# Weight sums of the Winograd product made ahead and kept in DRAM, operand low parts on GpSimd, operand sums on VectorE

## What is computed

```python
def sq_relu_mlp(h, w1, w2):
    return jnp.square(jax.nn.relu(h @ w1)) @ w2

xl = xl + g2_l * sq_relu_mlp(modulate(rms_norm_2(xl, norm2_g[i]), sh2_l, s2_l),
                             mlp_w1[i], mlp_w2[i])
return rms_norm_2(xl, final_g)
```

## Time and profile before

| | us |
|---|---|
| median of 3 runs | 2065.61 (2061.8 to 2067.92) |
| the profiled execution, its own time | 2060.92 |
| its span on the core | 2058.9 |
| TensorE, matmuls, busy | 1984.6 |
| VectorE / ScalarE / GpSimd busy | 1236.4 / 861.5 / 924.2 |
| second product, groups 0 to 6 | from 1667.4 to 2002.8 |

### The profile page before, as it was taken

The page is one execution under the profiler, slowest core; times in us unless marked ns, Lnnn a source line. Parts: engine busy times, 40 slices in busy tenths (PEclk is TensorE's granted clock), DMA queues, the critical chain, the costliest instruction groups (busy, mean ns, idle before and its releaser), DMA issues.

```text
span 2058.9 us, 26605 instructions
## 1 busy us (share of the span) xinstructions
PE 1984.6 (96%) x10042; PEld 1658.4 (81%) x10042; DVE 1236.4 (60%) x2117; ACT 861.5 (42%) x1431; POOL 924.2 (45%) x562
## 2 busy tenths in 40 slices
PE   9999999999999999999999999999999998888897
PEld 7988988988988888888878877787888876666676
DVE  6255355536554455554789978974402058888866
ACT  5433332253435513122465575756445443333321
POOL 4512111221122335344279856883447466666621
PEclk9999999999999999999999999999999999999998
DMA  4301101111113677684354423443354432222222
GB/s 184 103 21 52 52 21 62 42 42 42 37 47 108 227 274 271 218 295 132 113 187 181 174 93 120 127 141 124 108 180 152 139 133 87 82 82 92 82 92 82
DMA packets 82814, 247.11 MB, mean 120 GB/s; under 512 B 9328, under 2 KB 9712, under 8 KB 82560
## 3 DMA queue, kind: packets, MB, share of 16 engines
q1 hardware_dynamic: 59504, 202.94, 29.0%
q10 hardware_dynamic: 23184, 42.48, 5.7%
...
## 4 chain that ended last, share of the span: by engine, by line
PE 51%; DVE 8%; issue 4%; POOL 3%; ACT 2%; DMA 1%; POOLq 0%; DVEq 0%; ACTq 0%
PE B L1711 34%; PE B L1890 9%; PE B L1941 5%; DVE RES L2478 2%; DVE OPL L2475 2%; DVE SUMR L2475 2%; DMA RAW<-wall 1%; POOL WL L3041 1%; POOL SUML L3046 1%; PE B L2016 1%; DVE HB L2478 1%; PE B L1952 0%; POOL CO L3107 0%; POOL OPT L3057 0%; DVE B L2478 0%
## 5 line engine op out<-in xcount | busy, mean ns | idle before, releaser
L1711 PE MATMUL B<-HB,WH 128*128 128x512 f32 x2976 | 948.9, 401 | 4.9 <-ACT HB L2141 2.2
L1711 PEld LDWEIGHTS B<-HB,WH 128*128 128x128 f32 x2976 | 547.6, 189 | 127.0 <-issue 17.1
L3041 POOL TENSOR_TENSOR WL<-RAW,WH 128x1024 fp32r<-128x1024 f32 x160 | 389.6, 2439 | 457.8 <-ACT WH L2141 367.4
L1711 PE MATMUL B<-HB,WL 128*128 128x512 f32 x1488 | 578.2, 391 | 1.0 <-POOL WL L3041 1.0
L2141 ACT ACTIVATE WH<-RAW 128x1024 fp32r<-128x1024 f32 x201 | 210.8, 1054 | 297.1 <-DMA RAW<-wall 267.2
L1711 PEld LDWEIGHTS B<-HB,WL 128*128 128x128 f32 x1488 | 280.0, 188 | 61.7 <-POOL WL L3041 1.9
L3037 POOL TENSOR_TENSOR WL<-RAW,WH 128x512 fp32r<-128x512 f32 x82 | 113.9, 1413 | 315.0 <-ACT WH L2141 314.9
L2478 DVE SCALAR_TENSOR_TENSOR B<-UP,vec,B 128x512 f32<-128x512 f32 x308 | 206.2, 746 | 0.0
L2478 DVE SCALAR_TENSOR_TENSOR RES<-B,modv,RES 128x512 f32<-128x512 f32 x204 | 150.2, 742 | 64.2 <-PE B L1941 27.1
L1774 PE MATMUL B<-WH,HB 128*128 128x256 f32 x768 | 153.2, 297 | 0.0
L3027 POOL TENSOR_TENSOR small<-small 128x4 f32<-128x4 f32 (+2 forms) x36 | 38.4, 1068 | 211.4 <-DVE small L2481 211.1
...
## 6 DMA issues: line engine op xcount, KB each, us to landing
RAW<-wall SPq DMA_DIRECT2D x200, 512.0 KB, 3.6
MODRAW<-wmod ACTq DMA_DIRECT2D x96, 256.0 KB, 4.7
WH<-parts SPq DMA_DIRECT2D x32, 512.0 KB, 3.2
WL<-parts SPq DMA_DIRECT2D x32, 512.0 KB, 4.2
hscr<-HR ACTq DMA_DIRECT2D x64, 256.0 KB, 3.0
HQ<-hscr SPq DMA_DIRECT2D x32, 512.0 KB, 4.7
RES<-xT SPq DMA_DIRECT2D x16, 512.0 KB, 7.6
oscr<-OT SPq DMA_DIRECT2D x32, 256.0 KB, 2.1
```

Source lines behind the costliest of these rows:

```text
L1711: i = pe.matmul(bank, a[:, ks], hb(part, k, h), start=k == 0 and n == 0, stop=k == 7 and n == 2)
L3041: i = po.tensor_tensor(lo, raw, hi.bitcast(F32), ALU.subtract)
```

## The change

Four things. (1) The sums S1 to S4 of all 28 units are made in the hidden stage: one unit per hidden tile is loaded from DRAM into SUMW, summed by VectorE, and stored to a DRAM buffer `sums` (512 KB in, 512 KB out). In the second product `sum_load` reads them back, three buffers ahead, and `sum_split` makes SUMH and SUML. (2) The RAW unit of the second product is 768 columns wide (A11, A12, A22; A21 occurs in sums only), for its load, WH and WL. Quarters are contiguous (the host lays them out). (3) `op_sum` moves from GpSimd to VectorE. (4) `operand`, the low part OPL, moves from VectorE to GpSimd. The first three `sum_load`s and `sum_split(0)` stand after the last hidden tile; a sum_load waits for the last store of its class n mod 3 and, for n > 2, for the parts 3, 5, 6, 7 of unit n - 3. The semaphores d_mod become d_side and are used again.

```diff
         q = split[0]
         while loaded[0] <= q:
             u_load()
-        if is_summed(UNITS[q]):
-            for t in SUMS:
-                piece("w_sum", q, t)
         if not is_split(UNITS[q]):
             piece("split", q)
         split[0] += 1
...
             piece("operand", q, m)
             yield
+    def sums_ahead():
+
+        for n in range(4 * LAST + 2):
+            if n < 4 * LAST:
+                piece("s_load", n)
+            if n > 1:
+                piece("s_store", n - 2)
+            yield
+            if 0 < n <= 4 * LAST:
+                for t in SUMS:
+                    piece("w_sum", n - 1, t)
+            yield
+
+    def sum_load(n):
+        if n < 4 * LAST:
+            piece("sum_load", n)
+
+    def sum_split(n):
+        piece("sum_split", n)
+
     ahead_of = operands_ahead(0)
+    sums = sums_ahead()
     for i in range(GT, 4 * HG):
         hidden(i, 1)
...
+        next(sums, None)
+        next(sums, None)
         if i > GT + 2:
             next(ahead_of, None)
             next(ahead_of, None)
     for _ in ahead_of:
         pass
+    for _ in sums:
+        pass
+    for n in range(3):
+        sum_load(n)
+    sum_split(0)
     first = UNITS.index(("w2", 0, 0, 2))
     def unit_ahead(n, place):
+        if place == 2 and n + 1 < 4 * LAST:
+            sum_split(n + 1)
+        if place == 5:
+            sum_load(n + 3)
         q = first + n + 2
         if q < split[0] or q >= n_units:
             return
-        if is_summed(UNITS[q]):
-            if place < 4:
-                piece("w_sum", q, SUMS[place])
-                return
         if place == 4:
             while loaded[0] <= q:
                 u_load()
...
+        def columns_of(q):
+
+            o = q % NW * 1024
+            return slice(o, o + 768) if q in SUMMED else slot(q)
...
         def quarter(t, a):
-            k, f = int(a[2]) - 1, int(a[1]) - 1
-            return t[:, 512 * k:512 * k + 512].rearrange("p (r c) -> p r c", r=2)[:, :, f * 128:f * 128 + 128]
+            o = QUARTERS[a]
+            return t[:, o:o + 256]
+
+        MOD_LOADS = [16 * len(range(i, 96, NMOD)) for i in range(3)]
+
+        def sums_done(n):
+
+            return MOD_LOADS[n % 3] + 32 * (n // 3 + 1)
+
+        def wait_sum_loaded(w, n):
+
+            w.wait_ge(sig[f"d_side{n % 3}"], sums_done(4 * LAST - 1 - (4 * LAST - 1 - n) % 3) + 16 * (n // 3 + 1))
...
-                        c = 512 * (int(a[2]) - 1) + 256 * r + 128 * (int(a[1]) - 1)
+                        c = QUARTERS[a] + 128 * r
...
-                copy(WH[:, slot(q)], RAW[:, slot(q)]).then_inc(sig[f"w_hi{q % NW}"], 1)
-                if q in SUMMED:
-                    n = SUMMED[q]
-                    w.wait_ge(sig["s_sum"], 4 * n + 4)
-                    copy(SUMH[n % 3][:, :], SUMR[n % 3][:, :]).then_inc(sig["s_hi"], 1)
+                c = columns_of(q)
+                copy(WH[:, c], RAW[:, c]).then_inc(sig[f"w_hi{q % NW}"], 1)
+
+            def sum_split(n):
+                wait_sum_loaded(w, n)
+                if n > 2:
+                    for m in (3, 5, 6, 7):
+                        wait_part(w, (n - 3) // 4, (n - 3) % 4, m)
+                copy(SUMH[n % 3][:, :], SUMR[n % 3][:, :]).then_inc(sig["s_hi"], 1)
...
-            def operand(q, m):
-                x = SLOT_OF[q, m]
-                w.wait_ge(sig["op_hi"], nth["operand", q, m])
+            def op_sum(q, m):
+                to = OPT[SLOT_OF[q, m]][:, :]
+                wait_operand_slot(w, q, m)
+                wait_hq(w, q)
                 if m == 5:
+                    i = tt(to, hq(q, "B12"), hq(q, "B11"), ALU.subtract)
+                elif m == 6:
+                    w.wait_ge(sig["op_sum"], nth["op_sum", q, 5])
+                    i = tt(to, hq(q, "B22"), raw_operand(q, 5), ALU.subtract)
+                elif m == 4:
                     w.wait_ge(sig["op_sum"], nth["op_sum", q, 6])
-                elif m == 6:
-                    w.wait_ge(sig["op_sum"], nth["op_sum", q, 4])
-                tt(OPL[x][:, :], raw_operand(q, m), OPH[x][:, :].bitcast(F32), ALU.subtract).then_inc(sig["op_lo"], 1)
-
-            def w_sum(q, s):
-                n = SUMMED[q]
-                raw, to = RAW[:, slot(q)], SUMR[n % 3]
-                w.wait_ge(sig[f"d_raw{q % NW}"], 16 * raw_n[q])
-                if n > 2:
-                    m = next(m for m in TERMS if TERMS[m][0] == s)
-                    wait_part(w, (n - 3) // 4, (n - 3) % 4, m)
-                else:
-                    wait_full(w, "hid", GT - 1, 1)
-                two = sums_view(to, s).rearrange("p (r c) -> p r c", r=2)
+                    i = tt(to, hq(q, "B21"), raw_operand(q, 6), ALU.subtract)
+                else:
+                    i = tt(to, hq(q, "B22"), hq(q, "B12"), ALU.subtract)
+                i.then_inc(sig["op_sum"], 1)
+
+            def w_sum(n, s):
+                raw, to = SUMW[n % 3], SUMR[n % 3]
+                w.wait_ge(sig[f"d_side{n % 3}"], sums_done(n) - 16)
+                two = sums_view(to, s)
...
                 i.then_inc(sig["s_sum"], 1)
...
             def split(q):
-                raw, hi, lo = RAW[:, slot(q)], WH[:, slot(q)], WL[:, slot(q)]
+                c = columns_of(q)
+                raw, hi, lo = RAW[:, c], WH[:, c], WL[:, c]
                 w.wait_ge(sig[f"d_raw{q % NW}"], 16 * raw_n[q])
                 if q >= NW:
                     wait_unit_read(w, q - NW)
                     for c in (slice(0, 512), slice(512, 1024)):
                         i = po.tensor_tensor(lo[:, c], raw[:, c], hi[:, c].bitcast(F32), ALU.subtract)
                 else:
-                    if q in SUMMED:
-                        w.wait_ge(sig["s_sum"], 4 * SUMMED[q] + 4)
                     i = po.tensor_tensor(lo, raw, hi.bitcast(F32), ALU.subtract)
                 i.then_inc(sig[f"w_lo{q % NW}"], 1)
-                if q in SUMMED:
-                    n = SUMMED[q]
-                    w.wait_ge(sig["s_hi"], n + 1)
-                    po.tensor_tensor(SUML[n % 3][:, :], SUMR[n % 3][:, :], SUMH[n % 3][:, :].bitcast(F32),
-                                     ALU.subtract).then_inc(sig["s_lo"], 1)
-
-            def op_sum(q, m):
-                to = OPT[SLOT_OF[q, m]][:, :]
-                wait_operand_slot(w, q, m)
-                wait_hq(w, q)
+
+            def sum_split(n):
+                w.wait_ge(sig["s_hi"], n + 1)
+                po.tensor_tensor(SUML[n % 3][:, :], SUMR[n % 3][:, :], SUMH[n % 3][:, :].bitcast(F32),
+                                 ALU.subtract).then_inc(sig["s_lo"], 1)
+
+            def operand(q, m):
+                x = SLOT_OF[q, m]
+                w.wait_ge(sig["op_hi"], nth["operand", q, m])
                 if m == 5:
-                    i = po.tensor_tensor(to, hq(q, "B12"), hq(q, "B11"), ALU.subtract)
+                    w.wait_ge(sig["op_sum"], nth["op_sum", q, 6])
                 elif m == 6:
-                    w.wait_ge(sig["op_sum"], nth["op_sum", q, 5])
-                    i = po.tensor_tensor(to, hq(q, "B22"), raw_operand(q, 5), ALU.subtract)
-                elif m == 4:
-                    w.wait_ge(sig["op_sum"], nth["op_sum", q, 6])
-                    i = po.tensor_tensor(to, hq(q, "B21"), raw_operand(q, 6), ALU.subtract)
-                else:
-                    i = po.tensor_tensor(to, hq(q, "B22"), hq(q, "B12"), ALU.subtract)
-                i.then_inc(sig["op_sum"], 1)
+                    w.wait_ge(sig["op_sum"], nth["op_sum", q, 4])
+                po.tensor_tensor(OPL[x][:, :], raw_operand(q, m), OPH[x][:, :].bitcast(F32), ALU.subtract).then_inc(sig["op_lo"], 1)
...
-                    sp.dma_start(RAW[:, slot(q)], wall[WALL.index(contents(UNITS[q])), :, :]).then_inc(sig[f"d_raw{q % NW}"], 16)
+                    c = columns_of(q)
+                    sp.dma_start(RAW[:, c], wall[WALL.index(contents(UNITS[q])), :, 0:c.stop - c.start]).then_inc(sig[f"d_raw{q % NW}"], 16)
+
+            def s_load(n):
+                if n > 2:
+                    w.wait_ge(sig["s_sum"], 4 * n - 8)
+                else:
+                    wait_full(w, "hid", GT - 1, 1)
+                sp.dma_start(SUMW[n % 3][:, :], wall[WALL.index(("w2", n // 4, n % 4)), :, :]).then_inc(sig[f"d_side{n % 3}"], 16)
+
+            def s_store(n):
+                w.wait_ge(sig["s_sum"], 4 * n + 4)
+                sp.dma_start(sums[n, :, :], SUMR[n % 3][:, :]).then_inc(sig[f"d_side{n % 3}"], 16)
+
+            def sum_load(n):
+                w.wait_ge(sig[f"d_side{n % 3}"], sums_done(4 * LAST - 1 - (4 * LAST - 1 - n) % 3))
+                if n > 2:
+                    for m in (3, 5, 6, 7):
+                        wait_part(w, (n - 3) // 4, (n - 3) % 4, m)
+                sp.dma_start(SUMR[n % 3][:, :], sums[n, :, :]).then_inc(sig[f"d_side{n % 3}"], 16)
...
+            if u[1] < LAST:
+                t = t.reshape(128, 2, 2, 2, 128)
```

(1 more changed line is left out.)

27 lines of the change are left out of this document (15 added, 12 removed).

## The result

The changed kernel takes 2032.06 us (median of 4 runs, 2027.52 to 2035.19), the kernel before, beside it, 2065.11 us: a ratio of 0.9839, with a 95% interval of 0.9814 to 0.9864. That is 33 us faster, 8 us better than the forecast of 2040 and inside the range of 2014 to 2064. The profiled execution has a span of 2028.9 us against 2058.9, 30.0 us less.

The account below looks back on a forecast made before the run. TensorE, busy 96%, bounds the kernel; only the second product's 63.5 us loss was winnable. Loss after: start 12 + groups 26.4 + group 6's 2.8 = 41.2, so 22.3 us faster, 2038.6, put at 2040; range 2014 to 2064.

Parts of the forecast that it names:

- Loss per group: Second product: four operand-sum pairs delay evictions, costing TensorE 1.1 us each, 4.4 per group, a period of 42.5 us.
- cross-check by the port's sum plus 2.9 us: Second product: shared SBUF port work of 40.1 us per group plus today's excess of 2.9 gives a 43.0 us period.
- Group 6: Second product's group preparing raw quarters for the last group, with half the weight sums: keeps its loss of 2.8 us.
- Start gap: Second product's start: TensorE waits for unit 27's load, sums, store and reload; 12 us with slow clock, ends 8 and 18.
- Hidden stage: Extra sums, loads and stores cost 0: VectorE is idle there and DMA can carry the needed 337 GB/s.
- Rival E: Hidden stage binds on DMA and ends 8 us late: 2048 us, chance 0.07.
- GpSimd's low part: Second product: each of 14 low parts per group takes 1.28 us on GpSimd, 17.9 in all, making GpSimd's sum 34.7.
- Rival B: Second product: GpSimd becomes the bound, 45.4 us per group, gain only 5 us: 2057 us, chance 0.15.
- HQ loop of 38.1 us: Second product: next group's HQ load, waiting for m = 7's low part on GpSimd, loops in 38.1 us, inside 42.5.
- Rival C: Second product: late m = 7 low part delays HQ load, gaps pass 3.5 us each group: 15 us slower, 2077, chance 0.07.
- Rival D: Second product: moving work between port users gains nothing, 10.4 us per group stays; 12 us slower, 2074, chance 0.06.
- The clock: Second product's groups: no gap reaches 3.5 us, so the granted clock stays; only the start gap adds 1.7 to 2 us.

Follow-up runs that it names:

- experiment 8: Changed kernel with paired operand sums one preparation step apart and the low parts on VectorE too, leaving GpSimd only WL and SUML: 2040.02 us, ratio 0.9887.
- experiment 4: Changed kernel with the two operand sums of a pair one preparation step apart instead of next to each other, for m = 5, 6, 4: 2021.02 us, ratio 0.9798.
- Experiment 1: Changed kernel with the exchange of engines undone (operand sums on GpSimd, low parts on VectorE), weight sums still made ahead: 2040.97 us, ratio 0.9898.
- experiment 6: Changed kernel with one entry of operand work per hidden tile instead of two, spreading group 0's operands over more tiles: 2027.31 us, ratio 0.9833.
- experiment 7: Changed kernel with sums of units 0 to 2 made last and kept, paired operand sums apart, stores one tile later, first sum_split before the last hidden tile: 2007.79 us.
- experiment 9: The kernel of experiment 7 with one entry of operand work per hidden tile instead of two, as in experiment 6: 2004.16 us, ratio 0.9712.
- experiment 2: Kernel before with the exchange of engines alone (operand sums on VectorE, low parts on GpSimd), weight sums still in the second product: 2056.54 us, ratio 0.9975.
- experiment 10: The kernel of experiment 8 with each of GpSimd's weight instructions (WL, SUML) cut in two halves of the same total width: 2024.5 us, ratio 0.9815.

## Why the prediction was right, point by point

- **The bound, and where the gain is.** Right: the second product gave back 38.1 us, and no other stage gained.
- **Loss per group, forecast 4.4 us.** This step of the sum was mis-sized: 1.8 us. The working took four pairs of operand sums at 1.1 us each as equal. In the trace three of the four find time before their eviction and cost nothing, and one (m = 4), which meets an OPL and a SUML in turn, makes a group of 39.92 instead of 38.1, 1.8 us. A pair's delay had been put right (near 3.0 us; measured 4.20), but an average pair does not hold anything up: only the excess over the slack of one place counts. The cross-check by the port's sum plus 2.9 us, which gave 43.0, was no independent support: experiment 8 puts less on the port than experiment 4 and is slower, so that sum alone sets no period at these loads. It made 4.4 look safer than it was. The step is worth 6 x 2.6 = 15.6 us, more than the whole miss.
- **Group 6, forecast to keep 2.8 us.** It loses nothing now: 203 matmuls in 46.0 us. Experiment 1, where only the weight sums have left, keeps 0.8 of the 2.8, so most of it was weight sums as well.
- **Start gap, forecast 12 us with ends of 8 and 18.** Right in its chain: 14.3 us. With T the end of the last matmul of the hidden stage (1675.5), the load was issued at T - 5.0, as forecast. Unit 27's quarters were there 6.5 us later and not 3.5 to 4.5, and its four sums took 3.0 us instead of 1.7, so they were ready at T + 4.5 instead of T + 1.1; the store and the reload together then took 5.8 us instead of 7.6, so the reload was there at T + 10.3 instead of T + 8.7, and the first SUML at T + 13.9 instead of T + 12. The 2.3 us too little are this lateness and the clock after the gap (2.4 us instead of 1.7 to 2). The landing under load was put too short and the way to DRAM and back too long: two errors that partly cancel.
- **Hidden stage, forecast 0.** This is the step that failed: it costs 5.0 us. The text asked whether the DMA can carry 337 GB/s, and it can (376 in the window, 345 without any wait in experiment 6). It did not ask what stands behind `s_store` in SP's queue while that waits for VectorE, nor that sums of 0.42 us, on an engine "where it is idle", would take up to 2.67 us beside GpSimd's instructions. Both questions were asked of the second product and not of the stage that received the work. Rival E had the place and, at 8 us, near the size, but the wrong cause.
- **GpSimd's low part, forecast 1.28 us.** Measured 1.28 to 1.78 with a median of 1.30. The engine is busy 36.6 us a group, forecast 34.7. Rival B, GpSimd as the bound, is refuted by experiment 4: with GpSimd 96% busy the groups are within 0.3 us of packed.
- **HQ loop of 38.1 us inside the period.** It held: with groups of 38.1 to 38.4 us (experiments 4, 7 and 9) the largest distance between two starts in groups 1 to 5 is 0.73 us. Rival C did not come about.
- **Rival D, that moving between two users of the port gives nothing.** Refuted by the difference of experiment 1 and the changed kernel, 2.9 us a group, and nearly right for experiment 2, 1.0. The Trainium skill's rule that such a move might not help (Perfetto Trace Analysis, "Optimizing Scalar/DVE Operations") is thus neither wrong nor enough here: the same move gave 1.0 of 10.4 us lost per group with VectorE crowded, and 2.9 of 4.7 without.
- **The clock.** Behind the gap of 1.94 us in each group the granted clock stayed at 1.00, as forecast; before it was 0.96 over a group. But the reason given, that a gap must reach 3.5 us to cost clock, does not hold. In the kernel before the clock is 0.50 from 1905 to 1908 us, right behind a gap of 2.2 us; in experiment 9 it is 0.50 behind one of 2.3, in experiment 10 behind one of 2.2, while in experiment 7 it stays at 1.00 behind one of 2.2.

The forecast loss of 41.2 us came to 25.6: 15.6 us better than the sum, made of 15.6 in the groups and 2.8 in group 6, less 2.3 at the start and 0.5 that no term names. Against it stand 5.0 us in the hidden stage and 3.1 ahead of it, in work that the change does not touch. So the span fell by 30.0 us where 22.3 were forecast. The place and the direction were right by their reasons; that the time came within 8 us was in part luck, since errors of opposite sign covered each other.

Each blocked instruction agrees with what the Trainium skill says of the shared pair (SBUF — State Buffer, "Who interferes with whom"): a VectorE instruction with two SBUF inputs contends with a GpSimd instruction that reads SBUF. In these rows it ends 0.54 to 0.55 us after its neighbour where it is 128x512, and 0.28 us after it where it is 128x256.

Open: whether the store's place in the queue costs the whole kernel its 4 us could not be read from the total, since the first HR moved by 5 us from run to run. Why VectorE stays full in experiment 6 while the waits go, and what keeps experiment 10's groups at 40.2 us, above experiment 4's 38.4, is open too.

## What to carry to other kernels

An engine that frees buffers is not judged by its busy share, nor by the load of the port that it shares, but by the longest stretch of queued work between two of its deadlines, each instruction priced with the rest of the neighbour's instruction that it may meet. To shorten that stretch, part the instructions (experiment 4: 8 us, for a change of order only) or cut the neighbour's into pieces (experiment 10). And a stage that receives work gets the same questions as the one that is relieved, above all: what queues behind its stores.
